# Groups of two experts instead of four in an expert loop, and output projections moved at the end of a mixer

## The reference

```python
def expert_block(args):
    toks, e = args
    xb = x_pad[toks]
    hb = jax.nn.silu(xb @ w_gate[e]) * (xb @ w_up[e])
    return hb @ w_down[e]
...
y = jax.ops.segment_sum(y_blocks.reshape(P, D).astype(f32) * slot_w[:, None], slot_tok, num_segments=T + 1)[:T]

def hgrn2_mixer(h, w_in, lb, norm_g, w_out):
    ...
    o = o * lax.rsqrt(jnp.mean(o * o, axis=-1, keepdims=True) + EPS)
    o = o.reshape(B_, S, C_HEADS * C_DV) * norm_g.astype(f32) * jax.nn.silu(g.astype(f32))
    return o.astype(h.dtype) @ w_out
```

## Time and profile before

| | |
|---|---|
| median of 3 runs | 1595.73 us (1593.35 to 1598.78) |
| profiled execution, its own time | 1596.03 us |
| its span, from the first to the last instruction | 1593.6 us |
| mean granted TensorE clock | 0.994 of full speed |
| PE busy, PE's weight loads, DVE, ACT, POOL | 96%, 47%, 35%, 22%, 13% of the span |
| DMA | 471.97 MB, mean 296 GB/s |

### The profile page before, as it was taken

The page is one execution under the profiler, slowest core; times in us unless marked ns, Lnnn a source line. Parts: engine busy times, 40 slices in busy tenths (PEclk is TensorE's granted clock), DMA queues, the critical chain, the costliest instruction groups (busy, mean ns, idle before and its releaser), DMA issues. The chain is left out here.

```text
span 1593.6 us, 23381 instructions
## 1 busy us (share of the span) xinstructions
PE 1537.7 (96%) x9800; PEld 745.2 (47%) x9800; DVE 552.7 (35%) x1285; ACT 346.0 (22%) x577; POOL 210.4 (13%) x256
## 2 busy tenths in 40 slices
PE   7999999999999999988999999999999999999987
PEld 4444545544444444423566666645544444444422
DVE  4222636332222122125244444446332222122115
ACT  3131621100000000003444555432010000000003
POOL 5000000000000000000244444420000000000000
PEclk9999999999999999999999999999999999999999
DMA  8611056999999999997421112124999999999996
GB/s 314 247 62 53 27 229 273 409 367 426 428 427 427 427 426 427 427 422 316 185 81 54 54 62 95 58 95 183 375 360 427 427 426 427 427 427 428 426 422 275
DMA packets 59388, 471.97 MB, mean 296 GB/s; under 512 B 12929, under 2 KB 12937, under 8 KB 31376
## 3 DMA queue, kind: packets, MB, share of 16 engines
q1 hardware_dynamic: 54336, 462.51, 70.5%
q0 software_dynamic: 4800, 7.87, 1.3%
q10 hardware_dynamic: 144, 0.05, 0.0%
HBM read 452.03 MB, written 24.27 MB: 299 GB/s over the span
## 5 line engine op out<-in xcount | busy, mean ns | idle before, releaser
L827 PE MATMUL ps<-sb_ring,sb_work 128*56 128x512 f32 x2048 | 456.4, 598 | 21.1 <-issue 18.0
L827 PEld LDWEIGHTS ps<-sb_ring,sb_work 128*56 128x56 f32 x2048 | 147.6, 131 | 315.2 <-issue 314.8
L842 PE MATMUL ps<-sb_ring,sb_work 128*56 128x512 f32 x1024 | 230.9, 593 | 0.6 <-DMA sb_ring<-in_w_down_dram 0.6
L662 PE MATMUL ps<-sb_work,sb_h 128*64 128x224 f32 (+1 forms) x2304 | 218.1, 334 | 0.0
L1499 POOL DMA_INDIRECT expert_rows<-sb_work,sb_ri x60 | 54.9, 915 | 1118.2 <-DVE sb_work L1900 1105.5
L1891 DVE TENSOR_TENSOR sb_work<-sb_work,ps 56x512 f32<-56x512 f32 x64 | 69.3, 1083 | 336.3 <-ACT sb_work L1314 336.2
L662 PEld LDWEIGHTS ps<-sb_work,sb_h 128*64 128x64 f32 x2304 | 152.4, 137 | 63.9 <-issue 31.8
L1081 PE MATMUL ps<-sb_work,sb_ring 128*128 128x512 f32 x384 | 172.3, 603 | 2.0 <-ACT sb_work L1211 2.0
L1314 ACT ACTIVATE sb_work<-ps 56x512 f32<-56x512 f32 x64 | 37.7, 589 | 457.7 <-PE ps L827 457.7
L842 PEld LDWEIGHTS ps<-sb_ring,sb_work 128*56 128x56 f32 x1024 | 69.7, 130 | 119.4 <-issue 112.8
L1329 ACT ACTIVATE sb_work<-ps 56x512 f32<-56x512 f32 x60 | 35.5, 591 | 373.6 <-PE ps L842 373.6
(11 more groups left out here) (241 smaller groups left out, 1198.6 us busy)
## 6 DMA issues: line engine op xcount, KB each, us to landing
sb_ring<-in_w_down_dram SPq DMA_DIRECT2D x62, 2048.0 KB, 23.5
sb_ring<-in_w_gate_dram SPq DMA_DIRECT2D x54, 2048.0 KB, 21.0
sb_ring<-in_w_up_dram SPq DMA_DIRECT2D x54, 2048.0 KB, 25.7
sb_ring<-in_w_gate_dram SPq DMA_DIRECT2D x18, 1024.0 KB, 10.7
sb_ring<-in_w_up_dram SPq DMA_DIRECT2D x18, 1024.0 KB, 28.8
sb_ring<-in_c_w_in_dram SPq DMA_DIRECT2D x8, 2048.0 KB, 8.8
sb_ring<-in_ab_w_in_dram SPq DMA_DIRECT2D x5, 2048.0 KB, 11.4
expert_rows<-sb_work SPq DMA_DIRECT2D x2, 4096.0 KB, 20.6
```

Source lines behind the costliest of these rows:

```text
L662: mm = nc.tensor.matmul(dst[64 * z:64 * z + 64], a[:, 64 * z:64 * z + 64], b, start=start, stop=stop)
L827: mm = nc.tensor.matmul(dst[64 * z:64 * z + CAP, :], me["xgT"][:, j, c, q * CAP:(q + 1) * CAP], wblock(slots[z], NC)[:, c, :], start=(c == ...
L842: mm = nc.tensor.matmul(dst[64 * z:64 * z + CAP, :], src[:, c * CAP:(c + 1) * CAP], wblock(slots[2], FC)[:, c, z * 512:(z + 1) * 512], sta ...
```

## The change

PICK becomes 2: the loop works on groups of two experts, a pick has 112 columns, and each of the two experts of a group carries half of the next group's pick (four chunks, one bank of two): 16 steps, 10 before the turn and 6 behind it. The "second" jobs and `first_experts` go. Before the loop the first two experts are picked as before, but by two banks with four chunks each. Experts 0 and 1 carry group 1's pick, whole, between turn and down. The slot table moves behind expert 2's gate and up. `selections` makes two experts' matrices at the end of every second expert, behind that expert's output rows. The last group, experts 30 and 31, is picked within `last_experts`. `sel`, the scratch row `junk`, `late_pick`, `hT_odd` and `diag` get other places in the same buffer.

In mixer 1's last step (H = 9) the four matmuls of head 6's part go before `head_out(7)` and three of the seven parts of tile 0 before `head_sum(7)`; four are left behind the loop.

```diff
-PICK = 4
+PICK = 2
+PB = 2
+CB = NC // PB
...
@@ plan_moe
             for g in range(NE // PICK):
-                for b in range(4):
+                for b in range(PB):
                     bk.add(("pick", l, g, b), moe_bank(l, b))
-                if g == 0:
-                    for b in range(4):
-                        bk.add(("second", l, b), moe_bank(l, b))
...
@@ PE
-            def first_experts(l):
-
-                first_gate_up(l)
-                for e in range(2):
+            def expert(l, e):
+
+                g, q = e // PICK, e % PICK
+                if e >= 2:
+                    three = EXPERT_SLOTS[e % 3]
+                    for s, k in e_in[l * NE + e][0:2]:
+                        pe.wait_ge(ring_in[s], 16 * k)
+                    opens(("gu", l, e))
+                    if q == 0:
+                        for b in range(PB):
+                            wait_drained(pe, ("pick", l, g, b))
+                    mm = gate_up(l, three, g % 2, q, range(0, 4))
+                    if e == 2:
+                        mm.then_inc(gu_half, 1)
+                    fills(gate_up(l, three, g % 2, q, range(4, 8)), ("gu", l, e))
+                    if e == 2:
+                        slot_table(l)
+                    pick(l, g + 1, q, range(0, 10))
                     turn(l, e)
-                    pick_first(l, e, part=1)
-                    out_rows(l, e)
-                pick_first(l, 2, part=1)
-                pick_first(l, 3, part=1)
-                slot_table(l)
...
+                    pick(l, g + 1, q, range(10, 16))
                 else:
...
+                    turn(l, e)
+                    pick(l, g + 1, q, range(0, 16))
                 out_rows(l, e)
...
@@ last_experts
                 last_gate_up(l, a, range(0, 8))
+                pick(l, NK // PICK, 0, range(0, 16))
                 last_gate_up(l, b, range(0, 4))
                 last_turn(l, a)
                 last_gate_up(l, b, range(4, 8))
+                pick(l, NK // PICK, 1, range(0, 16))
                 last_down(l, a, range(0, 3))
...
                 more_blocks(l)
+                for n in range(PB):
+                    wait_drained(pe, ("pick", l, NK // PICK, n))
...
@@ mixer 1
+                    if k == 0 and H == HEADS_C + 1:
+                        pe.wait_ge(y_ready, HEADS_C - 1)
+                        for t in range(NT):
+                            out_part(1, w1_in[8], m1["y"], t, 0, HEADS_C - 2)
                     if k == 0 and H >= 2:
                         head_out(H - 2)
+                    if k == 1 and H == HEADS_C + 1:
+                        for c in range(3):
+                            out_part(1, w1_in[9], m1["y"], 0, 1, c)
                     if k == 1 and H >= 2:
                         head_sum(H - 2)
...
-            pe.wait_ge(y_ready, HEADS_C - 1)
-            for t in range(NT):
-                out_part(1, w1_in[8], m1["y"], t, 0, HEADS_C - 2)
-            for c in range(HEADS_C - 1):
+            for c in range(3, HEADS_C - 1):
                 out_part(1, w1_in[9], m1["y"], 0, 1, c)
...
@@ DVE, dve_expert
                 if e == 0:
                     hidden(l, 1)
+                take_pick(l, g + 1, q)
                 if e == 1:
                     slot_lists(l)
-                    for b in range(4):
-                        take_first(l, b, 1)
                     row_table(l)
-                if 2 <= e < NE - PICK:
-                    for b in {2: (0,), 3: (1, 2, 3)}.get(e, (q,)):
-                        take_pick(l, g + 1, b)
...
@@ DVE, last_experts
                 last_turned(l, a)
+                take_pick(l, NK // PICK, 0)
                 last_hidden(l, b)
                 last_turned(l, b)
+                take_pick(l, NK // PICK, 1)
```

More of the change, by code:

```diff
@@ L695, in positions, with pick_first @@
                 fills(mm, ("pos", l, t))
-            def pick_first(l, t, cs=range(NC), part=0):
+            def pick_first(l, t, cs=range(NC)):
                 pe.wait_ge(sel_ready, (l * (NE // PICK + 3)) + t + 1)
-                n = 2 * CAP
+                n = PICK * CAP
                 for c in cs:
-                    job = ("second", l, c // 2) if part else ("pick", l, 0, c // 2)
-                    if t == 0 and c % 2 == 0:
+                    job = ("pick", l, 0, c // CB)
+                    if t == 0 and c % CB == 0:
                         opens(job)
-                    mm = halves(bank(job)[:, (c % 2) * n:(c % 2 + 1) * n], h_cols(t, c),
-                                hx["sel"][:, t, part * n:(part + 1) * n], t == 0 and c % 2 == 0, t == NT - 1 and c % 2 == 1)
-                    if t == NT - 1 and c % 2 == 1:
+                    mm = halves(bank(job)[:, (c % CB) * n:(c % CB + 1) * n], h_cols(t, c), hx["sel"][:, t, :],
+                                t == 0 and c % CB == 0, t == NT - 1 and c % CB == CB - 1)
+                    if t == NT - 1 and c % CB == CB - 1:
                         fills(mm, job)
             def pick(l, g, b, steps):
-                job = ("pick", l, g, b)
+                job, n = ("pick", l, g, b), PICK * CAP
                 if steps[0] == 0:
@@ L863, in first_gate_up @@
                     for b in range(4):
-                        if e == 0:
-                            wait_drained(pe, ("pick", l, 0, b))
+                        if e == 0 and b % 2 == 0:
+                            wait_drained(pe, ("pick", l, 0, b // 2))
                         mm = gate_up(l, EXPERT_SLOTS[e], 0, e, (2 * b, 2 * b + 1), 6 if e else 7)
@@ L924, in expert @@
                 out_rows(l, e)
-                if e == 2:
-                    pick(l, 1, 1, range(0, 8))
             def last_gate_up(l, e, cs):
@@ L1053, in moe @@
                 pick_first(l, 3)
-                first_experts(l)
-                for e in range(2, NS):
+                first_gate_up(l)
+                for e in range(NS):
                     expert(l, e)
@@ L2079, in moe @@
             def moe(l):
-                for b in range(4):
-                    take_first(l, b, 0)
+                for b in range(PB):
+                    take_pick(l, 0, b)
                 selections(l, 1)
```

58 lines of the change are left out of this document (15 added, 43 removed).

## The result

The changed kernel takes 1599.88 us (median of 20 runs, 1597.93 to 1602.19), the kernel before 1595.22 (20 runs, 1593.35 to 1601.13). The ratio is 1.0025, 95% interval 1.0018 to 1.0032: slower by 4 us. By its middle value that is inside the 0.3% that I called no change; the upper end of the interval is just outside. The forecast was 1600.0. The profiled execution took 1600.28 us by its own time, with a span of 1598.6 us, 5.0 over the span before.

A forecast was written before the change was run, and what follows sets the result against it. It took DMA to bound the expert loop at 427 GB/s, with PE having about 1.1 us to spare per expert. Its terms 2.2 + 2.2 + 0.9 - 1.0 = +4.3 us gave a median of 1600.0 us, range 1591 to 1605.

The forecast's parts named there:

- Price of the picks: Steady expert loop: one expert's picks stay at 3.0 to 3.2 us, at most 0.2 us more per expert, costed at nothing.
- The rival with the picks bound by their weight loads: Expert loop: 112-column records take as long as 224-column ones, 1695 us, or some 1653 by the skill's page; chance 0.02.
- Path to expert 3's gate and up: PE's early experts in each layer: fewer picks -2.8, idle wait +4.0, lowered clock +1.8, together +3.0 us.
- The wait: PE behind the slot table at expert 2, idle until DVE's selections come: 4.0 us once per layer.
- The clock: Pick behind PE's new idle time at expert 2: the lowered clock adds 1.8 us.
- From the issue to the stream: Expert 6's gate load, issued later, shifts the stream of loads by 2.0 to 3.0 us; 2.2 taken in each layer.
- Nothing later gives it back: Behind expert 6's gate load the stream is full, so the 2.2 us shift lasts to the end of each layer.
- The ends of the layers: Group 15's picks in the last experts: nothing in layer 0, between 0 and 1.9 us in layer 1, 0.9 taken.
- Mixer 1: End of mixer 1: two idle times filled, -1.89 us, one new wait of 0.9 us, net -1.0 us.
- No lowered clock: Rival at expert 2: PE's new wait is there but doesn't lower the clock, total +1.1 us, 1597; chance 0.14.
- No wait: Rival at expert 2: DVE has the selections before PE asks, the stream's hole closes, total -5.8 us, 1590; chance 0.12.
- Late in both ends: Rival in the last experts: PE comes late in both layers, total +7.4 to 9 us, 1603 to 1605; chance 0.14.

The follow-up runs named there:

- e7_delay4: The kernel before with four unread 512-column matmuls in front of expert 2's gate and up in each layer: 1603.79 us, ratio 1.0056.
- e8_delay8: The kernel before with eight unread 512-column matmuls in front of expert 2's gate and up in each layer: 1611.96 us, ratio 1.0097.
- e3_busywait: The changed kernel with four unread 512-column matmuls where PE waits for the selections: 1597.15 us, ratio 1.0016.
- e4_no_last_picks: The changed kernel without group 15's picks in the last experts and their takes, so the output misses a part: 1598.69 us, ratio 1.0021.
- e9_order_part1: e1_order with one part of tile 0 ahead of mixer 1's head sum instead of three: 1590.62 us, ratio 0.9974 against the kernel before.
- e1_order: The changed kernel with DVE's selections right behind the slot lists and the row table after expert 2's hidden product: 1592.23 us, ratio 0.9972.

## Why the prediction was right

**What bounds the kernel.** Right. The steady loop stayed at 427 GB/s, with more records on PE and no more time, and lateness on the path up to expert 3's gate and up lengthened the layers. e7_delay4 and e8_delay8 show it by themselves.

**Price of the picks.** Right: 3.11 us for the picks of one expert in the trace of after, for 3.0 to 3.2 forecast, and 13.92 us for an expert. The rival with the picks bound by their weight loads fell, and with it the estimate by the Trainium skill ("TensorE: Matmul & The Clock Gate", section on the back-to-back issue gap). By that rule 64 records take 5.2 us; at full clock they took 3.1 here.

**Path to expert 3's gate and up.** Forecast -2.8 + 4.0 + 1.8 = +3.0, measured +2.70, of which 0.27 arose ahead of the layer's G, where the first takes before the loop are twice as wide. The prediction had counted nothing there. From G it is +2.43. Its terms:
- The wait: 4.0 forecast, 3.79 measured (3.75 in layer 1), with the releaser that was named.
- The clock: 1.8 forecast, measured 3.61 - 2.09 = 1.5 (2.09 is what 40 such records take later in the loop), 1.47 by e3_busywait, and 3.77 - 2.09 = 1.7 in layer 1. This term was somewhat too large, and the working shows why. I took the loss as 5.18 - 3.43 and 12.21 - 10.3, which sets a duration, with the way through the array in it, against a distance of starts. By durations alone it is 5.18 - 3.65 = 1.5 and 12.21 - 10.51 = 1.7 (10.51 is the row of after).
- What is left is 2.43 - 3.79 - 1.52 = -2.9, forecast -2.8.

**From the issue to the stream.** Forecast 2.2 of a range of 2.0 to 3.0, as the landing time was open. In layer 0 the load landed 2.63 us later from G, and the stage took 2.82 more. I had weighted the 7.7 of layer 1 over the 8.7 of layer 0 for no good reason; the load needed 8.9 us in layer 0 and 7.4 in layer 1, so each layer kept its own. In layer 1 the landing came 2.25 later, as forecast. The same slip made layer 0 too small by 0.6.

**"Nothing later gives it back".** Borne out in layer 0, not in layer 1, and this step was wrong there. The reason given was that from there on the stream is full, and in layer 1 of before it wasn't: 322 and 328 GB/s in two windows. The lateness of 2.25 us at expert 6's gate was -0.3 at expert 7's, and layer 1 grew by 0.94 us only, for 2.2 + 0.9 forecast. The two delays show the same, each with some 2 us missing in layer 1. That the sum of the landings still meets the medians is thus in part luck.

**The ends of the layers.** At the branch behind expert 29 PE is 1.96 us late in layer 1, by the difference of 1553.27 to 1547.25 less the 4.06 by which the layer started late; +1.9 was forecast. It then came out at the lower bound: the 48 records took 10.51 us at full clock, where before they took 12.21, and PE then waited 0.58 us for down weights. In the kernel before there was no such wait, so DMA, not PE, ended last here, and the lateness of PE was gone. My term of 0.9 is not resolved by the times: e4_no_last_picks gives 1.2 with overlapping intervals. A cost of 4 us (the rival's 1596) is outside them.

**Mixer 1.** Forecast -1.0, measured -0.81 in the trace. The wait was 0.74 us for 0.9 forecast. But an idle time of the profile starts at a modelled end: by the starts the stop took 0.90, and without it (e9_order_part1) the stretch is 1.01 shorter. The last 0.1 is not traced.

**Not foreseen.** The lowered clock before a layer's first gate and up, 1.7 us. In this pair of executions it stands before layer 1 of after only; in all traces it comes in 8 of 22 such places, before and after the change. So the agreement of 1600.28 with the forecast of 1600.3 is partly luck and better than the steps deserve: layer 0 was 0.6 low, layer 1 2.2 high, and 1.8 that I had not counted stood between. The medians, which mix executions with and without it, lie at +4.7 for +4.3 forecast. The direction and most of the size rest on what was shown, the wait, the clock and the late issue.

**The rivals.** "No lowered clock" is e3_busywait: 1597 forecast, 1597.15 measured. "No wait" is e1_order: 1590 forecast, 1592.23 measured; the price of 2.8 and 2 us for a closed hole may have been too high, as in the three kernels with this issue the load landed 0.4 to 3.1 us sooner. "Late in both ends" needed lateness of 1.6 us in layer 0's last stage; there PE stood waiting for a load as before (0.97 us at 718.32, before 0.99).

## What to carry to other kernels

When work is regrouped, go through the in-order queue of the engine that makes the inputs. Here a small step (the row table) that waits for PE stood ahead of what PE needed next, and moving one line turned 4.7 us of loss into 3 to 4 us of gain. Where a stream of loads bounds a loop, find the last load that is issued into a hole. Lateness up to that issue was paid in full in layer 0, and some 2 us less in layer 1: look whether the stream behind it is really full, in each layer, before you say that nothing gives it back. Price an idle time of TensorE with two terms, the idle time and what the lowered clock takes from the instructions behind it. And where one profiled execution of each kernel is compared, look for a lowered clock in places that the change didn't touch.

## What the hardware showed that I had not expected

- An idle time of about 2 to 3 us does not decide whether the clock falls. It stayed at full speed behind 2.67 (e4_no_last_picks) and 3.09 us (after), and fell behind 2.26 (e4_no_last_picks), 2.63 and 3.17 us (before). Behind the same 2.01 or 2.02 us ahead of a layer's first gate and up it fell in 8 of 22 places. It fell behind 3.79 and 3.75. By durations against those at full clock the loss was 1.5 to 1.7 us in the rows shown, except behind 2.26 us, where 46 records took 12.16 us for some 10.1 at full speed (10.51 x 46 / 48), 2.1 lost.
- A stop of 0.74 us by the profile in a run of 512-column matmuls was 0.90 us by the starts.
- Time from issue to landing of the same load differs between the layers: 8.7 and 8.9 us in layer 0, 7.7 and 7.4 in layer 1 (before, after), and 8.5 to 9.1 and 7.4 to 7.8 in all kernels that issue it no earlier than before and whose profile shows its landing. The transfer itself would take 4.9 at 427 GB/s. Issued 3.0 us earlier it took 8.6 to 10.3 in both layers.
